# Stick-breaking attention with a running product of sigmoids in place of cumulative sums of logarithms

## The reference

```python
def stick_breaking_attention(q, k, v):
    """A[t,s] = sig(z_ts) * prod_{s<j<t} (1 - sig(z_tj)), s < t."""
    for i in range(seq // SB_BLOCK):        # 4 blocks of 128 queries
        z = jnp.einsum("bhqd,bhkd->bhqk", qb, kb) * scale
        valid = s_pos < t_pos
        log_1m = jnp.where(valid, jax.nn.log_sigmoid(-z), 0.0)
        log_a = jax.nn.log_sigmoid(z) + lax.cumsum(log_1m, axis=3, reverse=True) - log_1m
        a = jnp.where(valid, jnp.exp(log_a), 0.0)
        outs.append(jnp.einsum("bhqk,bhkd->bhqd", a.astype(v.dtype), v[:, :, :kend]))
```

## Time and profile before

| what | value |
|---|---|
| median of 3 runs | 1806.93 us (1806.84 to 1809.66) |
| own time of the profiled execution | 1808.46 us |
| its span, first to last instruction | 1806.4 us |
| mean granted TensorE clock | 0.987 |
| PE busy, share of the span | 1742.8 us, 96% |
| DVE busy | 914.6 us, 51% |
| ACT busy | 690.0 us, 38% |
| POOL busy | 171.4 us, 9% |

### The profile page before, as it was taken

How to read it: one execution, slowest core, us unless ns; L and a number is a source line. 1 busy time by engine, 2 the same in 40 slices (tenths; PEclk the granted TensorE clock), 3 DMA queues, 4 the chain that set the end, 5 groups by cost and what they waited for, 6 DMA issues and landing times.

```text
span 1806.4 us, 19361 instructions
## 1 busy us (share of the span) xinstructions
PE 1742.8 (96%) x7808; PEld 1369.1 (76%) x7808; DVE 914.6 (51%) x1264; ACT 690.0 (38%) x989; POOL 171.4 (9%) x202
## 2 busy tenths in 40 slices
PE   7999889999999999999999999999999999999999
PEld 6776667676877866888888887777765788888887
DVE  5334644354446344444444233877655577777421
ACT  4243225354335233422323234425565444444211
POOL 2010001021111000100000022122111200000000
PEclk9999989999999999999999999999999999999999
DMA  6221112121342322233223223141122223333221
GB/s 232 94 82 54 51 48 77 63 82 48 105 152 93 118 70 86 89 99 100 93 94 102 97 93 105 60 175 59 59 59 82 82 94 104 94 95 104 93 94 58
DMA packets 47304, 164.29 MB, mean 91 GB/s; under 512 B 5024, under 2 KB 5152, under 8 KB 46896
## 3 DMA queue, kind: packets, MB, share of 16 engines
q1 hardware_dynamic: 46032, 158.88, 26.7%
q0 software_dynamic: 896, 3.70, 0.6%
q10 hardware_dynamic: 288, 0.48, 0.1%
HBM read 158.81 MB, written 4.23 MB: 90 GB/s over the span
## 4 chain that ended last, share of the span: by engine, by line
PE 87%; DVE 6%; ACT 4%; issue 2%; DMA 1%; POOL 0%; SPq 0%; ACTq 0%; DVEq 0%; POOLq 0%
PE pst L353 87%; ACT WH L874 1%; ACT L879 1%; DVE WL L1473 1%; DVE ee L1648 0%; PE pst L755 0%; DVE zs L1646 0%; DMA raw<-wst 0%; DMA X<-xT 0%; DVE qx L1700 0%; DVE ZL L1481 0%; ACT ZH L874 0%; POOL spt L2185 0%; DVE XL L1485 0%; ACT ee L874 0%
## 5 line engine op out<-in xcount | busy, mean ns | idle before, releaser
L353 PE MATMUL pst<-XH,WH 128*128 128x512 f32 x1320 | 529.5, 401 | 2.1 <-ACT v L874 1.6
L1473 DVE TENSOR_TENSOR WL<-raw,WH 128x1024 fp32r<-128x1024 f32 x277 | 345.4, 1247 | 352.3 <-ACT WH L874 351.9
L353 PE MATMUL pst<-XL,WH 128*128 128x512 f32 x1320 | 515.7, 391 | 0.0
L353 PE MATMUL pst<-XH,WL 128*128 128x512 f32 x1320 | 515.4, 390 | 0.0
L874 ACT ACTIVATE WH<-raw 128x1024 fp32r<-128x1024 f32 x277 | 291.0, 1051 | 364.4 <-PE pst L353 359.5
L353 PEld LDWEIGHTS pst<-XH,WH 128*128 128x128 f32 x1320 | 248.9, 189 | 68.5 <-issue 14.7
L353 PEld LDWEIGHTS pst<-XH,WL 128*128 128x128 f32 x1320 | 248.8, 188 | 52.7
L353 PEld LDWEIGHTS pst<-XL,WH 128*128 128x128 f32 x1320 | 249.2, 189 | 51.9 <-issue 2.9
L353 PE MATMUL pst<-HH,WH 128*128 128x512 f32 x352 | 139.2, 396 | 0.0
L353 PE MATMUL pst<-HL,WH 128*128 128x512 f32 x352 | 139.2, 396 | 0.0
L353 PE MATMUL pst<-HH,WL 128*128 128x512 f32 x352 | 139.2, 396 | 0.0
(11 more groups left out here) (251 smaller groups left out, 1982.7 us busy)
## 6 DMA issues: line engine op xcount, KB each, us to landing
raw<-wst SPq DMA_DIRECT2D x277, 512.0 KB, 3.6
X<-xT SPq DMA_DIRECT2D x8, 512.0 KB, 7.6
xs<-X SPq DMA_DIRECT2D x1, 2048.0 KB, 8.9
nC<-cd POOLq DMA_DIRECT2D x4, 512.0 KB, 8.6
X<-xs SPq DMA_DIRECT2D x2, 1024.0 KB, 5.5
outT<-X SPq DMA_DIRECT2D x8, 256.0 KB, 4.5
qx<-memT SPq DMA_DIRECT2D x1, 1024.0 KB, 4.9
gt<-cd POOLq DMA_DIRECT2D x1, 1024.0 KB, 4.9
```

The costliest lines, as they stand in the source:

```text
L353: return nc.tensor.matmul(out, lhs, rhs, start=start, stop=stop)
L1473: vec.tensor_tensor(WL[:, i % NHL, :], raw[:, i % NRAW, :], WH[:, i % NHL, :].bitcast(F32), ALU.subtract).then_inc(wl, 1)
```

## The change

Scores are made with queries on the partitions, two heads of a pair at a time, for query block i (3, 2, 1, 0) and all its `w = (i + 1) * 128` keys. ScalarE takes sigmoid(-z) into `pb` and sigmoid(z) into `sg`, both heads in one instruction, straight from the two banks. GpSimd puts 1 and 0 into what is not valid in the diagonal block. VectorE makes one running product per head along the keys, from the last to the first (`tensor_tensor_scan` in place over a reversed access pattern), and multiplies `sg` by it, shifted by one. TensorE transposes the weights by block into the banks of the scores, ScalarE copies them to `pb`, TensorE multiplies by v into bank `b0`, and ScalarE copies the 128 query columns of both heads into `q`. There are 16 such units (4 pairs, 4 blocks) of 5 steps, in four streams of 20. The main stream has twice as many steps: TensorE stops in a tile after two, four and six of eight slices (`cuts=(1, 3, 5)`; `fine=True` for zv), the other engines take each step as two (`twice`). The gate step of VectorE in the first two branches waits in addition for its own eighth `y_ok`.

The four parts of the diff under the new order are TensorE, ScalarE, VectorE and GpSimd, in this order.

```diff
+def twice(g):
+    for _ in g:
+        yield
+        yield
...
-        zs = sb("zs", [P, 2, 1280], stack=st)
-        spt = sb("spt", [P, 2, 1280], stack=st)
-        ee = sb("ee", [P, 2, T], stack=st)
+        pb = sb("pb", [P, 2, 2, T], stack=st)
+        sg_ = sb("sg", [P, 2, 2, T], stack=st)
...
-        mixer_steps = 8 + 4 * 2 + 4 * 6 + 4 * 2 + 24 + 24
-        mixer_order = weave({"main": (0, 1, mixer_steps), "stick0": (0, 1, 4 * 22), "stick1": (0.004, 1.004, 4 * 22)}, {})
+        mixer_steps = 2 * (8 + 4 * 2 + 4 * 6 + 4 * 2 + 24 + 24)
+        mixer_order = weave(
+            {"main": (0, 1, mixer_steps), "stick00": (0.02, 0.5, 20), "stick01": (0.5, 0.97, 20), "stick10": (0.04, 0.53, 20), "stick11": (0.53, 1.0, 20)},
+            {("stick01", 0): (("stick00", 20),), ("stick11", 0): (("stick10", 20),)})
...
+            def stick(s, pn):
+                b0, b1, pt = 4 + 2 * s, 5 + 2 * s, 2 * s + pn
+                for x, i in enumerate((3, 2, 1, 0)):
+                    n, w = 4 * pn + x, (i + 1) * P
+                    free(b0)
+                    free(b1)
...
+                    for e in range(2):
+                        po = 64 * e
+                        ins = mm(ps[b0 + e][:, 0:w], q[po:po + 64, pt, i * P:(i + 1) * P], kk_[po:po + 64, pt, 0:w])
+                    ins.then_inc(s_sc[s], 1)
+                    yield
+                    yield
+                    yield
+                    pe.wait_ge(s_d[s], 3 * n + 3)
+                    for e in range(2):
+                        for j in range(i + 1):
+                            ins = nc.tensor.transpose(ps[b0 + e][:, j * P:(j + 1) * P], sg_[:, s, e, j * P:(j + 1) * P], ident)
+                    ins.then_inc(s_tr[s], 1)
+                    yield
+                    pe.wait_ge(s_a[s], 4 * n + 3)
...
+                    for e in range(2):
+                        h = 2 * pt + e
+                        for j in range(i + 1):
+                            ins = mm(ps[b0][64 * e:64 * e + 64, 0:P], v[:, j, h * 64:(h + 1) * 64], pb[:, s, e, j * P:(j + 1) * P], j == 0, j == i)
+                    ins.then_inc(s_pv[s], 1)
+                    hold[b0], hold[b1] = (s_a[s], 4 * n + 4), (s_a[s], 4 * n + 3)
+                    yield
...
+                    yield
+                    table(SIGMOID)
+                    act.wait_ge(s_sc[s], n + 1)
+                    act.wait_ge(s_pv[s], n)
+                    run(ACT.Sigmoid, pb[:, s, :, 0:w], z, scale=-1.0).then_inc(s_a[s], 1)
+                    run(ACT.Sigmoid, sg_[:, s, :, 0:w], z).then_inc(s_a[s], 1)
+                    yield
+                    yield
+                    act.wait_ge(s_tr[s], n + 1)
+                    run(ACT.Copy, pb[:, s, :, 0:w], z).then_inc(s_a[s], 1)
+                    yield
+                    act.wait_ge(s_pv[s], n + 1)
+                    run(ACT.Copy, q[:, pt, i * P:(i + 1) * P], ps[b0][:, 0:P]).then_inc(s_a[s], 1)
+                    yield
...
+                        dve.wait_ge(y_ok, 8)
...
+                    yield
+                    yield
+                    dve.wait_ge(s_g[s], 2 * n + 1)
+                    for e in range(2):
+                        back = pb[:, s, e, w - 1::-1]
+                        vec.tensor_tensor_scan(back, back, back, 1.0, ALU.mult, ALU.bypass).then_inc(s_d[s], 1)
+                    dve.wait_ge(s_d[s], 3 * n + 2)
+                    dve.wait_ge(s_g[s], 2 * n + 2)
+                    vec.tensor_tensor(sg_[:, s, :, 0:w - 1], sg_[:, s, :, 0:w - 1], pb[:, s, :, 1:w], ALU.mult).then_inc(s_d[s], 1)
+                    yield
+                    yield
+                    yield
...
+                    yield
+                    for c, (buf, fill) in enumerate(((pb, 1.0), (sg_, 0.0))):
+                        B = buf[:, s, :, i * P:(i + 1) * P]
+                        pool.wait_ge(s_a[s], 4 * n + c + 1)
+                        gp.affine_select(out=B, in_=B, compare_op=ALU.is_gt, fill=fill, base=0, pattern=[[0, 2], [-1, P]], channel_multiplier=1).then_inc(s_g[s], 1)
+                    yield
+                    yield
+                    yield
+                    yield
```

More of the change, by code:

```diff
@@ L445, in branch @@
                         b = ring()
-                        yield from tile(f"mix{n}", b, XH, XL)
+                        yield from tile(f"mix{n}", b, XH, XL, cuts=cuts)
                         hold[b] = (gs, 8 * nth + 2 * mp + e + 1)
@@ L465, in mixer @@
                     b = ring()
-                    yield from tile("zu", b, XH, XL)
+                    yield from tile("zu", b, XH, XL, cuts=cuts)
                     hold[b] = (u_ok, m + 1)
@@ L471, in mixer @@
                         b = ring()
-                        yield from tile("conv", b, XH, XL)
+                        yield from tile("conv", b, XH, XL, cuts=cuts)
                         hold[b] = (cv, 7 * m + (1, 2, 6)[x])
@@ L528, in stick @@
                     ins.then_inc(s_pv[s], 1)
-                    hold[b0] = (s_a[s], 13 * hn + 13)
+                    hold[b0], hold[b1] = (s_a[s], 4 * n + 4), (s_a[s], 4 * n + 3)
                     yield
-            follow(mixer_order, {"main": mixer(), "stick0": stick(0), "stick1": stick(1)})
+            follow(mixer_order, {"main": mixer(), **{f"stick{s}{n}": stick(s, n) for s in range(2) for n in range(2)}})
             drain(branch(2, 0, 0, 12))
@@ L1014, in mixer @@
                 yield from branch(1, 2)
[L1016 to L1020, removed]
-                    yield
[L1022 to L1039, removed]
-                    yield
@@ L1042, in act_program, with stick @@
-            follow(mixer_order, {"main": mixer(), "stick0": stick(0), "stick1": stick(1)})
+            def stick(s, pn):
+                b0, pt = 4 + 2 * s, 2 * s + pn
+                for x, i in enumerate((3, 2, 1, 0)):
+                    n, w = 4 * pn + x, (i + 1) * P
+                    z = pst[:, b0:b0 + 2, 0:w]
+                    yield
+                    table(SIGMOID)
[3 more added lines that the diff above has]
+                    run(ACT.Sigmoid, sg_[:, s, :, 0:w], z).then_inc(s_a[s], 1)
+                    yield
+                    yield
[5 more added lines that the diff above has]
+                    yield
@@ L1043, in act_program @@
+            follow(mixer_order, {"main": twice(mixer()), **{f"stick{s}{n}": stick(s, n) for s in range(2) for n in range(2)}})
             act.wait_ge(mm_, DONE["mix1", "branch", 7])
             for m in range(4):
-                act.wait_ge(s_a[m // 2], 26 * (m % 2) + 26)
+                act.wait_ge(s_a[m // 2], 16 * (m % 2) + 16)
                 run(ACT.Copy, YH[0][:, m, :], q[:, m, :]).then_inc(sph, 1)
@@ L1634, in mixer, with stick @@
                 yield from branch(1, 2)
-            def stick(s):
-                E = ee[:, s, :]
-                for hn in range(4):
+            def stick(s, pn):
+                for x, i in enumerate((3, 2, 1, 0)):
+                    n, w = 4 * pn + x, (i + 1) * P
                     yield
[L1640 to L1658, removed]
-                    yield
-            follow(mixer_order, {"main": mixer(), "stick0": stick(0), "stick1": stick(1)})
+                    yield
+                    dve.wait_ge(s_g[s], 2 * n + 1)
[8 more added lines that the diff above has]
+                    yield
+            follow(mixer_order, {"main": twice(mixer()), **{f"stick{s}{n}": stick(s, n) for s in range(2) for n in range(2)}})
             for m in range(4):
```

64 lines of the change are left out of this document (10 added, 54 removed).

## The result

The changed kernel takes 1736.26 us in the median of 4 runs (1733.93 to 1737.55), the kernel before beside it 1808.3 us: ratio 0.9598, 95% interval 0.9580 to 0.9616.

A forecast was written before the change was run, and what follows sets the result against it. The prediction took TensorE, busy for 96% of the span, as the bound, with its waits and low clock. Its terms summed to -62.4 us, from 1806.9 to 1745 us (1744.5), range 1736 to 1767.

The forecast's parts named there:

- Cumulative sums and transposes: TensorE, first mixer: removing the cumulative sums saves 34.6 us, eighty added transposes cost 8.7 us.
- Scores: TensorE, first mixer: a pair's two heads stand back to back and run at once, -8.5 us, bounds 0 and -8.5.
- Value products: TensorE, first mixer: 80 passes of 128 columns cost 1.2 us more than before, bounds 0 to +1.2.
- Breaks: TensorE's main stream: 48 breaks in place of some 36, 0.28 us each, +3.4 us, bounds 0 and +4.
- Waits and clock: TensorE, first mixer: waits on spt go, -23.0 us, and the low clock behind them, -14.6 us.
- New waits: TensorE in the new chain: 3 us of waits and 2 for the clock, +5 us, bounds 0 and 37.6.
- Room: Between scores and transposes: three steps, 21 us, hold a chain of 6.2 us at the widest.
- My second reckoning: VectorE's queue: up to 8 us in a step of 7.2 us, so the four widest units may delay TensorE a microsecond.
- The wait did not move to the transposes: First rival: TensorE's wait moves to the transposes, kernel at 1767 us, or 1778 at worst; chance 0.13.
- Scores do overlap: Second rival, claiming the opposite: scores do not overlap (+8.5 us), breaks at upper bound, kernel at 1754 us; chance 0.08.
- The reversed scan costs what the forward one does: Third rival, claiming the opposite: a slow reversed scan makes VectorE the bound, 1833 us at 13 us a scan; chance 0.03.
- the rule: GpSimd reading SBUF and VectorE with two SBUF inputs block each other; could add 2.5 us to the chain.

The follow-up runs named there:

- score_split: Changed kernel with the score of a pair's second head one stick step after the first's; 1751.08 us, stage 303.4 us.
- Old_room: Kernel before, same arithmetic, with one more stick step between softplus and cumulative sums (26 steps a head, not 22); 1779.94 us, stage 336.3 us.
- load4: Changed kernel plus four unused 512-column VectorE products before the scans of every unit, 2.8 us a unit; 1765.67 us, stage 318.6 us.
- load4_room6: Changed kernel with four unused VectorE products a unit and six steps a unit in place of five; 1758.16 us, stage 313.8 us.

## Why the prediction was wrong

The sign, the mechanisms and most of the terms were right; the gain was 70.6 us of span, 71.1 of the stage, where the sum had 62.4. Two terms failed: the value products and the breaks. By its steps:

- **Cumulative sums and transposes:** -25.9 us forecast at full clock. The transposes took 7.7 us, not 8.7. Right to 1 us; the difference is the last pass of each group, which takes 0.03 us where a main matmul follows.
- **Scores:** -8.5 forecast, -8.3 measured, and score_split shows the overlap: apart they cost 10.0 us more, 1.3 of it by breaks.
- **Value products, the first term that failed.** Forecast +1.2, with bounds 0 and +1.2, from rows with 128-wide weights; measured -2.3. The heads write different halves of the array's columns and overlap where they meet, which the rows that I chose cannot show, because those heads use all columns. The lower bound was put at "nothing" with no reason against a gain. 3.5 us.
- **Breaks, the second.** Forecast +3.4, with bounds 0 and +4, from 36 against 48 at one price; the trace has 44 and 40. The old streams did not stand in pairs as often as I assumed, the new ones met more often. The price of 0.28 us, read around a score, was right for scores and value products, but breaks around cumulative sums and transposes are nearly free. By the distances, 22 breaks that end in scores or value products became 26, and the nearly free ones went from 21 to 14: about +1 us (an estimate from those counts and prices, 1.7 where every longer last pass is counted), so the term was 2 to 2.5 us too high. The order could have been counted step by step.
- **Waits and clock:** -23.0 and -14.6 forecast. The trace has 30.7 us of low clock before, so 15.4 lost, and 24.1 us from start to start in the seven waits, with 1.6 us more for zs that I left out. Old_room shows this part by itself at 27.4 us with some waits left, load4 that the two come back together (24.0 us of waits and 20.5 of low clock).
- **New waits:** +5 forecast with their clock; measured 5.0 of waits and 3.4 us of low clock (1.7 lost), 6.7. Near, but for the wrong reason: only 1.1 of it was for VectorE's product; 3.9 was for ScalarE's copies, for which the sum had nothing. The 2.2 us for q stand behind the spatial gate's copy.
- **Room, a step that held by luck.** I set 21 us between scores and transposes against a chain of 6.2. That was no measure: each engine comes to its part only at its own step, and in the trace the product ends 0 to 5.6 us before the transposes. My second reckoning, 8 us of work and lag in a step of 7.2, was the right one; load4 shows how near the edge it was.

The two failed terms make some 6 us of the stage's miss of 8.7. Waits and clock, old less new, were 1.2 us more than the sum had; the rest, 1 to 2 us, I can't assign. The range failed with them: its low end gave the new waits and the extra breaks back, but allowed no gain in the value products. Even their own lower bound, 0, was left out of it; with it the low end would have been 1734.9 us, against the measured 1734.3.

**The rivals.** The wait did not move to the transposes (1.1 us); with 2.8 us more a unit it does, as load4 shows. Scores do overlap. The reversed scan costs what the forward one does. GpSimd's selects do wait at times, as the rule said that I had weighed against the change (the Trainium skill, SBUF — State Buffer, Summary: rules for kernel authors). The changed kernel's trace agrees with it:

```profile
343.14 2.04 DVE L1465 TENSOR_TENSOR WL<-raw,WH 128x1024 fp32r<-128x1024 f32 x1 [0.41 <-ACT WH L872]
344.06 1.40 POOL L2202 TENSOR_SCALAR_AFFINE_SELECT pb<-pb 128x256 f32<-128x256 f32 x1
...
322.36 0.69 DVE L1532 TENSOR_TENSOR misc<-misc,pst 128x512 f32<-128x512 f32 x1 [1.27 <-PE pst L359]
322.42 0.41 POOL L2202 TENSOR_SCALAR_AFFINE_SELECT pb<-pb 128x256 f32<-128x256 f32 x1
```

Of its 32 selects 20 took 404 to 414 ns. The other twelve took 655 to 1399 ns; each of them began while VectorE ran an instruction with both inputs in SBUF, and ended 0.27 us after it (0.20 after a scan). Beside a VectorE instruction with one input in PSUM, as at 322.42, a select was not longer. No wait of TensorE is put down to a select; whether the longer ones delayed a product that TensorE waited for is open.

## What to carry to other kernels

Where engines run in order and share a woven schedule, the room between a producer's step and its consumer's decides, not the grain of the steps, and not the sum of the chain against all steps between: one more step there gave 27 us without touching the arithmetic. It helps only until the next queue is the tight one, as load4_room6 shows. When such waits go, most of the low clock behind them goes too, so count both. And before forecasting, count the breaks of the order exactly, price them by what stands in them, and give a term a lower bound below nothing unless a row excludes a gain: small matmuls of two heads on different halves of the array may overlap even when nobody asked for it.

## What the runs showed of the hardware

- Two matmuls whose weights are 64 columns wide and whose results go to partitions 0 to 63 and 64 to 127 start 6 to 7 ns apart and run at once when they are issued in turn, as two with 64 rows do; with one head's eight passes issued before the other's, the distances fit four of the second's beginning beside the first's. Sixteen passes of 128 columns took 1.58 us so, 1.09 us in turn.
- A scan over a reversed pattern in place costs what a forward one does: 1208 and 1225 ns for 512 columns; 430 ns for 128.
- 45 us more work on an engine that is busy for 153 of 293 us made the stage 26 us longer.
- A break in a stream of fp32r matmuls of 512 columns cost 0.29 us with float32 scores in it (64 rows of weights), 0.30 with float32 value products (64 columns), and 0.01 with transposes of 128 by 128.
- GpSimd's selects of 128x256 took 404 to 414 ns, and up to 1399 where they began beside a VectorE instruction with two inputs in SBUF; they then ended 0.20 to 0.27 us after it.
